# A two-block fp32 transformer on one core: forget sums inside the projection, context and gate constants loaded a phase ahead, two alternating semaphore sets, norms on 128 columns

## The reference, cut to what matters

```python
def rms_norm(x, gain):
    return x * lax.rsqrt(jnp.mean(x * x, -1, keepdims=True) + EPS) * gain

def first_block(x, ...):                      # DEPTH = 2 layers
    for l in range(DEPTH):
        h = rms_norm(x, g_pre); p = h @ w_in  # 1024 -> 6144 + 8
        ...   # three kinds of attention: differential (4 heads), stick-breaking (8), forgetting (8)
        ya = rms_norm(o, sub_gain) * (1.0 - lambda_init)        # per head, 128 features
        cum_log_f = jnp.cumsum(log_sigmoid(ff + f_bias), -1)    # forgetting attention's bias
        y = concat([ya, yb, yc]) @ w_out      # 1536 -> 1024
        x = x + rms_norm(y, g_post)

def second_block(x, ctx, ...):                # layer 0: hyena, layer 1: window attention
    for layer in range(2):
        h = rms_norm(lat, norm1) * (1 + mod[1]) + mod[0]    # the same for the context
        lat = lat + mod[2] * mixer(h)
        h = rms_norm(lat, norm2) * (1 + mod[4]) + mod[3]
        lat = lat + mod[5] * expert_choice_ffn(h)           # 16 experts, softmax router, top_k
    return rms_norm(lat, final_norm)
```

## Time and profile before

| | |
|---|---|
| median of 3 runs | 3804.66 us (3802.55 to 3804.95) |
| the profiled execution's own time | 3799.08 us |
| its span, first to last instruction | 3797.3 us |
| mean granted TensorE clock | 0.955 of full speed |
| PE busy | 3450.7 us, 91% of the span |
| DVE / ACT busy | 1242.7 us (33%) / 657.0 us (17%) |
| DMA, mean of the 16 engines over the span | 155 GB/s |

### The profile page before, as it was taken

How to read it: one execution, slowest core, us unless ns; L and a number is a source line. 1 busy time by engine, 2 the same in 40 slices (tenths; PEclk the granted TensorE clock), 3 DMA queues, 4 the chain that set the end, 5 groups by cost and what they waited for, 6 DMA issues and landing times. The chain is left out here.

```text
span 3797.3 us, 33327 instructions
## 1 busy us (share of the span) xinstructions
PE 3450.7 (91%) x13514; PEld 1577.6 (42%) x13514; DVE 1242.7 (33%) x2281; ACT 657.0 (17%) x1420; POOL 0.2 (0%) x4
## 2 busy tenths in 40 slices
PE   7999788999989799898977699999998998699998
PEld 3444343344344344454745433333333553333332
DVE  1110672111084334753564312121224572211112
ACT  1000441000053211110111211111002261111111
POOL 0000000000000000000000000000000000000000
PEclk9999999999999899999978899999999999799999
DMA  3333101233300212101311177767782102299995
GB/s 145 133 133 150 72 1 70 96 133 133 152 26 23 79 69 94 47 23 51 143 46 46 76 299 282 274 266 267 291 307 97 45 1 98 116 420 420 420 419 233
DMA packets 86528, 588.05 MB, mean 155 GB/s; under 512 B 12440, under 2 KB 13371, under 8 KB 15972
## 3 DMA queue, kind: packets, MB, share of 16 engines
q1 hardware_dynamic: 78624, 572.56, 38.2%
q10 hardware_dynamic: 7748, 13.30, 1.0%
HBM read 583.73 MB, written 2.10 MB: 154 GB/s over the span
## 5 line engine op out<-in xcount | busy, mean ns | idle before, releaser
L453 PE MATMUL ps<-mem 128*128 128x512 f32 x1152 | 506.8, 599 | 17.1 <-DVE mem L570 17.1
L1672 PE MATMUL ps<-mem 128*64 128x512 f32 x2048 | 467.4, 599 | 1.3 <-ACT mem L1619 0.7
L453 PEld LDWEIGHTS ps<-mem 128*128 128x128 f32 x1152 | 219.2, 192 | 301.4 <-issue 298.3
L1024 PE MATMUL ps<-mem 128*128 128x512 f32 (+1 forms) x768 | 253.0, 492 | 7.7 <-ACT mem L879 7.7
L1672 PEld LDWEIGHTS ps<-mem 128*64 128x64 f32 x2048 | 137.1, 137 | 291.1 <-issue 287.6
L1641 DVE SCALAR_TENSOR_TENSOR mem<-ps,mem 128x512 f32<-128x512 f32 x128 | 96.1, 751 | 359.4 <-PE ps L1601 356.7
L1024 PEld LDWEIGHTS ps<-mem 128*128 128x128 f32 x768 | 147.2, 192 | 113.7 <-issue 102.1
L797 PE MATMUL ps<-mem 128*128 128x512 f32 x384 | 167.1, 592 | 0.0
L450 PE MATMUL ps<-mem 128*128 128x512 f32 x384 | 167.0, 594 | 0.0
L1291 PE MATMUL ps<-mem 128*128 128x512 f32 (+1 forms) x384 | 142.2, 532 | 7.3 <-POOLq L174 7.3
L514 ACT ACTIVATE mem<-ps 128x512 f32<-128x512 f32 x48 | 28.7, 598 | 688.0 <-PE ps L453 688.0
(11 more groups left out here) (294 smaller groups left out, 3941.9 us busy)
## 6 DMA issues: line engine op xcount, KB each, us to landing
mem<-in_moe_w SPq DMA_DIRECT2D x384, 1024.0 KB, 7.9
mem<-in_w_in SPq DMA_DIRECT2D x48, 1024.0 KB, 9.1
mem<-in_ada_w SPq DMA_DIRECT2D x48, 1024.0 KB, 6.7
mem<-in_hy_w_in SPq DMA_DIRECT2D x24, 1024.0 KB, 6.4
mem<-in_w_out SPq DMA_DIRECT2D x12, 1024.0 KB, 8.9
mem<-in_k_win_l SPq DMA_DIRECT2D x8, 1024.0 KB, 6.9
mem<-in_hy_w_out SPq DMA_DIRECT2D x8, 1024.0 KB, 6.6
mem<-in_sw_w_in SPq DMA_DIRECT2D x6, 1024.0 KB, 5.8
```

Source lines behind the costliest of these rows:

```text
L453: m = mm(ps[:, j % 4, :], Wc[s][:, k, t * P:(t + 1) * P], HTL[:, k, :], start=(k == 0), stop=(k == KD - 1))
L1024: m = mm(ps[:, j % 4, 0:L], Wc[s][:, k, (j % 4) * P:(j % 4 + 1) * P], H[:, k, :], start=(k == 0), stop=(k == KD - 1))
L1672: m = mm(ps[64 * x:64 * x + 64, pair, :], lat(k), w[x][:, k % 4, :], start=(k == 0), stop=(k == KD - 1))
```

## The change

Six things change in the code.

1. **Sums in 32-row groups.** `pe_sums` splits a row of 512 tokens into four blocks of 128 columns and writes each to its own 32 partitions (for 256 tokens: two blocks, 64 partitions each). Root and reciprocal then take 128 columns. `pe_spread` multiplies one partition of each group by a row of ones, which puts each block's factors on all 128 partitions of a PSUM bank of its own, and the DVE's multiplications read them from these four (two) banks.
2. **The head norm** follows the new form: one sum phase after output block 4, spreads after blocks 6 and 7 into banks 0 to 3, and PE waits for `h_ready` 4 before it writes bank 0 in the *first* group. `dve_hyb_out` first inverts all four heads and then waits for spread 4.
3. **Two semaphore sets.** Odd and even phases use sets `a` and `b`. An engine that ends a phase waits for `cleared` (the clearing of the set of the phase before), increments `arrived` and waits for `arrived >= 3 * phase`. POOL clears the set of the finished phase while the next one runs.
4. **No loop.** Both layers of the first block are written out.
5. **Loads a phase ahead.** The context is loaded in the output phase of the first block's last layer, and its own phase is gone; router, iota row and pairing matrix are loaded in the phase ahead of the gate (`act_load_gate`), and `pe_moe_a` and `pe_moe_d` no longer wait for them.
6. **`dve_forget_sums`** is called at tile 35 of 48 inside the projection.

```diff
 def end_phase(A):
     if A.last:
         A.e.wait_ge(*A.last)
+    if A.sems.phase:
+        A.e.wait_ge(A.sems["cleared"], A.sems.phase)
     A.e.sem_inc(A.sems["arrived"], 1)
-    A.e.wait_ge(A.sems["phase_open"], A.opened())
-    A.e.sem_inc(A.sems["resumed"], 1)
+    A.sems.phase += 1
+    A.e.wait_ge(A.sems["arrived"], 3 * A.sems.phase)
...
+def clear_last_phase(A):
+    A.e.wait_ge(A.sems["arrived"], 3 * (A.sems.phase + 1))
+    numbers = [sem.num for sem in A.sems.sets[A.sems.phase % 2].values()]
+    A.e.sem_clear(range(min(numbers), max(numbers) + 1))
+    A.e.sem_inc(A.sems["cleared"], 1)
...
         def act_norm(A, src, sq, rs, n, bank, turn):
             for k in range(0, KD, 2):
                 act(sq[:, k, :], src[:, k, :], ACT.Square).then_inc(A.mark("squares"), 1)
+            act_load_root(A)
             A.e.wait_ge(S["stat"], turn)
-            act(rs, ps[:, bank, 0:n], ACT.Sqrt, bias=eps_col, scale=1.0 / D).then_inc(A.mark("rstd"), 1)
+            act_root(A, rs[:, 0:P], ps[:, bank, 0:P], D)
...
-        def pe_norm(A, sq, n, bank, turn):
+        def pe_sums(bank, x, start, stop, at=0):
+            groups = x.shape[-1] // P
+            rows = P // groups
+            for g in range(groups):
+                m = mm(ps[rows * g:rows * g + rows, bank, at:at + P], ONES[:, 0:rows], x[:, g * P:(g + 1) * P],
+                       start=start, stop=stop)
+            return m
+
+        def pe_spread(A, rs, n, banks, at=0):
+            rows = P // (n // P)
+            for g, bank in enumerate(banks):
+                m = mm(ps[:, bank, at:at + P], ONES[rows * g:rows * g + 1, :], rs[rows * g:rows * g + 1, 0:P],
+                       start=True, stop=True)
+            m.then_inc(A.mark("spread"), 1)
...
+        def pe_norm(A, sq, rs, n, bank, turn, banks=None):
             for k in range(KD):
                 A.e.wait_ge(S["squares_v" if k % 2 else "squares"], (turn - 1) * 4 + k // 2 + 1)
-                m = mm(ps[:, bank, 0:n], ONES, sq[:, k, :], start=(k == 0), stop=(k == KD - 1))
+                m = pe_sums(bank, sq[:, k, :], k == 0, k == KD - 1)
             m.then_inc(A.mark("stat"), 1)
-        def dve_recip(A, rs, turn):
+            if banks:
+                A.e.wait_ge(S["inverted"], turn)
+                pe_spread(A, rs, n, banks)
+
+        def dve_invert(A, rs, turn):
             A.e.wait_ge(S["rstd"], turn)
-            nc.vector.reciprocal(rs, rs).then_inc(A.mark(), 1)
-            A.e.wait_ge(*A.last)
+            nc.vector.reciprocal(rs[:, 0:P], rs[:, 0:P]).then_inc(A.mark("inverted"), 1)
...
+                if j == 35:
+                    dve_forget_sums(A)
             dve_mod_cols(A, l, 2)
-            dve_forget_sums(A)
...
         def pe_hyb_out(A, st):
-            for h in range(4):
-                A.e.wait_ge(S["squares"], h + 1)
-                mm(ps[:, h, :], ONES, SQS[:, h, :], start=True, stop=True).then_inc(A.mark("stat"), 1)
...
-                    if n == 0 and b < 4:
-                        A.e.wait_ge(S["rstd"], b + 1)
+                    if n == 0 and b == 0:
+                        A.e.wait_ge(S["h_ready"], 4)
...
+                    if n == 0 and b == 4:
+                        for h in range(4):
+                            A.e.wait_ge(S["squares"], h + 1)
+                            m = pe_sums(0, SQS[:, h, :], True, True, at=h * P)
+                        m.then_inc(A.mark("stat"), 1)
+                    if n == 0 and b in (6, 7):
+                        for h in (0, 1) if b == 6 else (2, 3):
+                            A.e.wait_ge(S["inverted"], h + 1)
+                            pe_spread(A, RSH[:, h, :], T, HEAD_BANKS, at=h * P)
...
             pe_post_stat(A, KD - 1)
+            A.e.wait_ge(S["inverted"], 5)
+            pe_spread(A, RS, T, POST_BANKS)
             pe_next_stat(A, 4 + KD)
...
-        def act_hyb_out(A):
+        def act_hyb_out(A, l):
+            if l == DEPTH - 1:
+                A.e.dma_start(CT, a["ctx"]).then_inc(S["const_in"], 16)
...
         def dve_hyb_out(A):
             for h in range(4):
-                dve_recip(A, RSH[:, h, :], h + 1)
-                stt(QT[:, h, :], QT[:, h, :], SMALL[:, 8:9], RSH[:, h, :], ALU.mult, ALU.mult).then_inc(A.mark(), 1)
+                dve_invert(A, RSH[:, h, :], 1)
+            A.e.wait_ge(S["spread"], 4)
+            for h in range(4):
+                q = blocks(QT[:, h, :])
+                stt(q, q, SMALL[:, 8:9], spread(HEAD_BANKS, h * P), ALU.mult, ALU.mult).then_inc(A.mark(), 1)
...
+        def act_load_gate(A, m_):
+            e = A.e
+            e.dma_start(m_.RTR, a["moe_router_2"][m_.layer].rearrange("(k p) n -> p k n", p=P)).then_inc(S["const_in"], 16)
+            e.dma_start(m_.IO, a["k_iota"]).then_inc(S["const_in"], 16)
+            if m_.ctx:
+                e.dma_start(m_.PAIR, a["k_pair"]).then_inc(S["const_in"], 16)
...
         def pe_moe_d(A, m_, st):
-            A.e.wait_ge(S["const_in"], 16)
...
-            with e.Fori(0, DEPTH) as l:
+            for l in range(DEPTH):
```

More of the change, by code:

```diff
@@ L127, in take, with __init__, __getitem__ @@
         return a
+class Sems(dict):
+    def __init__(self):
+        super().__init__()
+        self.sets = ({}, {})
+        self.phase = 0
+    def __getitem__(self, name):
+        turn = self.sets[self.phase % 2]
+        return turn[name] if name in turn else super().__getitem__(name)
 class Engine:
@@ L137, in __init__ @@
         self.last = None
-        self.phase = 0
-        self.loop = None
+        sems.phase = 0
     def mark(self, sem=None):
@@ L145, in mark @@
         return self.sems[sem]
-    def opened(self):
-        self.phase += 1
-        self.counts = {}
-        self.last = None
-        return self.phase if self.loop is None else self.loop[0] * self.loop[1] + self.phase
-    def leave(self, turns):
-        self.phase += self.loop[1] * (turns - 1)
-        self.loop = None
 def end_phase(A):
@@ L203, in build @@
         S["stored"] = ctx.enter_context(nc.semaphore("stored"))
-        nums = []
-        for n in PHASE_SEMS:
-            S[n] = ctx.enter_context(nc.semaphore(n))
-            nums.append(S[n].num)
-        assert max(nums) - min(nums) == len(nums) - 1
-        S["_range"] = (min(nums), max(nums))
+        for turn, sems in zip("ab", S.sets):
+            for n in PHASE_SEMS:
+                sems[n] = ctx.enter_context(nc.semaphore(f"{n}_{turn}"))
+            nums = [x.num for x in sems.values()]
+            assert max(nums) - min(nums) == len(nums) - 1
         total = Map()
@@ L376, in dve_setup, with act_root, act_load_root @@
             end_phase(A)
+        def act_root(A, roots, sums, n):
+            act(roots, sums, ACT.Sqrt, bias=eps_col, scale=1.0 / n).then_inc(A.mark("rstd"), 1)
+        def act_load_root(A):
+            act(MISC[:, 4:5], MISC[:, 1:2], ACT.Sqrt).then_inc(A.mark(), 1)
         def act_norm(A, src, sq, rs, n, bank, turn):
@@ L879, in act_mod_norm, with dve_mod_norm @@
                 act(H[:, k, :], H[:, k, :], ACT.Identity, bias=mod(layer, which, k, n)).then_inc(A.mark("h_ready"), 1)
-        def dve_mod_norm(A, n, sq, rs, layer, which, norm, turn):
+        def dve_mod_norm(A, n, sq, rs, layer, which, norm, turn, banks):
             L, X, H = side(n)
@@ L887, in dve_mod_norm @@
             stt(g, sc, 1.0, gv(norm, layer * KD, KD), ALU.add, ALU.mult).then_inc(A.mark(), 1)
-            dve_recip(A, rs, turn)
+            dve_invert(A, rs, turn)
+            A.e.wait_ge(S["spread"], turn)
             for k in range(KD):
-                stt(H[:, k, :], X[:, k, :], g[:, k:k + 1], rs, ALU.mult, ALU.mult).then_inc(A.mark("scaled"), 1)
+                stt(blocks(H[:, k, :]), blocks(X[:, k, :]), g[:, k:k + 1], spread(banks), ALU.mult, ALU.mult)\
+                    .then_inc(A.mark("scaled"), 1)
             A.e.wait_ge(*A.last)
@@ L2234, in _ @@
             end_phase(A)
-            with e.Fori(0, DEPTH) as l:
-                A.loop = (l, H_PHASES)
-                st.enter(l, N_HYB)
+            for l in range(DEPTH):
                 pe_hyb_proj(A, st)
@@ L2264, in _ @@
             act_setup(A)
-            with e.Fori(0, DEPTH) as l:
-                A.loop = (l, H_PHASES)
+            for l in range(DEPTH):
                 act_hyb_proj(A, l)
                 act_attn(A)
-                act_hyb_out(A)
-            A.leave(DEPTH)
-            e.dma_start(CT, a["ctx"]).then_inc(S["const_in"], 16)
-            e.wait_ge(S["const_in"], 16)
-            end_phase(A)
+                act_hyb_out(A, l)
             for y in HYENAS:
```

170 lines of the change are left out of this document (72 added, 98 removed).

## The result

The changed kernel takes 3702.09 us (median of 4 runs, 3697.88 to 3707.81), the kernel before 3804.8 in the same comparison: a ratio of 0.9732, 95% interval 0.9715 to 0.9749, 102.7 us gained. The profiled execution took 3697.88 us, 101.2 less than that of before.

The account below looks back on a forecast made before the run. PE sets the end; its 346 us of idle time and half-speed stretches can be won. Gains of 12.3, 5.3, 5.8, 7.2 and 51.9 less 17.0 make 65.5 us, so 3804.66 becomes 3739 us, range 3706 to 3775.

Parts of the forecast that it names:

- Forget sums: Ahead of attention in each layer: moving them to tile 35 removes PE's idle time, 12.3 us gained.
- loop: At the turn between layers: ACT's idle 3.8 us behind PE's last sum goes away.
- barriers: At phase ends: 0.53 us falls to 0.15, 0.38 gained each; 5.3 us for 14 that no other term holds.
- pairing matrix: Ahead of expert work: loading it earlier gains 5.2 us in the last phase and 2.0 in layer 0.
- head norm's stall: Output product, each layer: PE idles 5.8 us for DVE's multiplications, part of 8.5 lost a layer, 17.0 in all.
- Context: Ahead of the first hyena sum: loading the context without its own phase gains 5.8 us.
- Gate loads: At the gates: earlier constants save the router's wait, 10.4 us, and ACT's issues, 2.5; with layer 0's pairing matrix, 14.9.
- The narrow norm: All norms: small sums cost 0.07 us warm, 0.10 cold, 4.5 and 6.4 a norm; norm sites together gain 51.9.
- Behind the product: Norm sums between and behind the output product's blocks, and the chain after them: 3.85 us gained a layer, 7.7 together.
- Latent norms: Norms of the latents: gains of 4.4 us in hyena, 4.9 at window attention's projection, 4.45 at the final norm.
- The clock: Rival: shorter norms keep PE at 1.2 GHz longer in eight products behind them, 14 us less gain, 3753; chance 0.08.
- The rival of fast sums: Norm sums run as fast as squares arrive, 0.04 us an instruction or less; 26 us more gain, 3713; chance 0.18.

Follow-up runs that it names:

- split product: The changed kernel with its output product reordered: blocks 4 to 7 of the first two chunks before blocks 0 to 3 of both; 3684.7 us.
- gate order: The split product kernel with PE's router matmuls for the latents moved ahead of the context's norm in the gates; 3680.0 us.
- fillers: The kernel with split product and gate order, plus matmuls of unused result in PE's waits around the norms; 3671.15 us.

## Why the prediction was wrong, point by point

*What bounds the kernel*: right. PE's waits and half-clock stretches were the place of the gain.

*Forget sums* (12.3; 11.0 by undoing it), *loop* (3.8 inside the turn; 3.6, an interval that holds 0), *barriers* (0.38 each; DVE now crosses a phase end with 0.17 us of idle time, where it had 0.56), *pairing matrix* (5.2 in the last expert phase; 5.4, since from DVE's last instruction to the first gather it was 5.55 us and is 0.14), *head norm's stall* (5.8; 5.76): right in mechanism and size. *Context* (5.8; 7.6 by medians, 3.5 to 5.3 on its stretch) was right within what can be told. *Gate loads* (14.9; 18.8) were some 4 us too low, because a faster norm also shortens what would have covered the transfer.

*The narrow norm*: the mechanism right, the term mis-sized; this is the step that failed. "I take 0.07 warm and 0.10 cold, 4.5 and 6.4 us a norm, because that is the small instruction less its tail": the rows gave a price for instructions one behind another, and were used for instructions side by side. Measured are 0.034 and 0.057, 2.26 and 3.64 us a norm; the forecast's own sign of being wrong, sums under 3.5 us, came true. The spread was taken at 0.13 warm to 0.24 cold, 1.3 to 1.8 us for eight: it takes 0.50 and 0.81, tail included. The price enters everywhere:

- Head norm: sums, spreads and switches were to cost 6.4 + 0.7 us a layer. By the rows above, 1.2 + 0.8 + 0.9 = 2.9 beyond the product's own matmuls. With the cold clock at 2.4 in place of 1.8, a layer loses 4.9 and not 8.5: 7 us of the 37.
- Behind the product, layer 0: sums 3.4 in place of 1.95 (0.31 on each of five sums between blocks, 1.9 behind the last), root to multiplication 2.1 for 1.45, last sum of the next norm 0.8 for 0.45, the turn 6.7 for 5.8 (10.09 to 3.42): 13.0 for 9.65.
- Latent norms: the final one 8.6 us for 4.45 (from the last product's end to the end of the span), window attention's 8.5 for 5.3 with its barrier (from the last expert product's end to the projection), with squares as the limit.

*The clock* as a rival (3753) wanted 1.7 us more lost in each product behind a norm. Over the first 24 matmuls of five such products the half clock cost 10.5 us before, and 9.8 and 10.1 in the changed kernel's two traces: nothing more. What the clock did elsewhere no step foresaw. The context's stage was granted more, 5.8 us, and window attention lost 2.8 us, where PE had 1.00 over the first 22 us before and 0.84 after.

*The rival of fast sums* (3713, chance 0.18) had the mechanism and, by its sum, nearly the size: it set 26 us more for the norms, and undoing them shows 25.6 more. That the two agree so closely is in part luck: it had put its 26 us at the sums alone, where spreads are a part of what was measured, and the measurement is good to some 4 us. The 11 us between 3713 and 3702 lie outside it. Some 4 are the gate loads; the profiled execution has 5.8 of clock more and, in window attention, 2.8 less. The rest is not accounted for. *Range*: its low end was to take in the bounds of the unknown costs. The fast end of the small matmul, 0.03, stood in the forecast's own text ("by columns would be 0.03") but the range ended 7 us below that rival, and held the fast sums only if nothing else went better than forecast.

*Straight-line code and one-partition spreads*, named as what could break the forecast, did not: PE's idle time at the former turn is 1.66 and 0.95 us, both ended by DVE and neither by waiting for instructions, and eight spreads take 0.50 us, where two full matmuls of 512 columns take 0.86.

The best kernel made here, split product, gate order and fillers, takes 3671.15 us, 31 less than the changed one. Its largest part, 17 us, comes from the one loss that the forecast had named.

## What to carry to other kernels

A row's price holds for its arrangement: before small matmuls are priced, ask whether the rows' neighbours share a column group as the new ones will, and carry the fast bound through every term that uses the price, the losses too. Where a change must stall PE because banks are taken, look for work on the other banks that can be drawn forward: here four blocks of the next chunk hid 5.7 us of DVE work at no cost. Where PE waits 1 to 3 us around each norm, compare the clock behind it; fillers of full matmuls that end just before the awaited result gained 8.9 us here in all; those that ended 5.36 us ahead left the sums as slow as before.

## What the hardware showed beyond the expected

- Four column groups of 32 rows: 0.034 us an instruction of 128 columns side by side, 0.077 to 0.093 one after another, at full clock; 0.057 side by side at half. So four side by side take 0.136 and 0.228 us, little more than a quarter of a full matmul of 512 columns (0.107 and 0.212, from 0.43 and 0.85): an estimate by columns from the row of the full matmul would have been 21% low at full clock and 7% at half.
- A full matmul of 512 columns takes 0.43 us, yet four of 128 into the same 32 rows take 0.31 in the head norm, 0.37 in a latent norm: the narrow form is cheaper even one behind another.
- A wait of given length does not fix the clock behind it, not even in one kernel. At the start of the latents' second hyena phase PE waited 3.12 us in both traces of the changed kernel; 32 matmuls then took 16.87 us in the first, 13.99 in the second:

```profile
1448.23 16.87 PE L1152 MATMUL ps<-mem 128*128 128x512 f32 x32 [3.12 <-remote]
```
```profile
1450.97 13.99 PE L1152 MATMUL ps<-mem 128*128 128x512 f32 x32 [3.12 <-remote]
```

The first ran its start at 1.2 GHz (the row below); in the second the clock is 1.00 from 1450.97 to 1464:

```profile
1448.30:1452.00 3.70, 3.70 (x5) 1.64 (x6) 2.65 (x8) 0.00 (x0) 0.00 (x0) 0.50 0.99 414
```
